# Block-sparse attention steps in a decoder layer: next logits placed behind the turn, keys and values fetched by separate transfers

## The chip, the cores and the metric

One core of a Trainium2 chip runs the kernel in one launch. Its engines work side by side and meet through semaphores: TensorE (PE, with its weight loads as PEld), VectorE (DVE), ScalarE (ACT), GpSimd (POOL) and SyncE (SP), which issues all transfers of this kernel; 16 DMA engines carry them. The metric is device time in microseconds (us), the median of several executions.

## What is computed

One layer of a hybrid decoder for a prompt of 512 tokens and for eight sequences of eight new tokens each (T = 576 rows in all), float32:

```python
xn = rmsnorm(x, ln1_g)
qa, ka, va, pb, gates = jnp.split(xn @ w_in, SPLIT_IN, axis=-1)
y_a = attend(qa, ka, va).reshape(B, T, WIDTH_A) @ w_br_a
y_b, wkv_new, shift_new = rwkv7_branch(pb, shift_prev, wkv0, mu, w0, w2, a0, a2, g2, k_k, k_a, r_k, lnx_g, lnx_b)
...
h = x + (g_a * y_a + g_b * y_b) @ w_o
u = rmsnorm(h, ln2_g) @ w_up
...
out = h + (jax.nn.silu(gt) * val) @ w_down
```

`attend` for the new tokens is block-sparse over a paged past of 4096 positions: for each head and token the 16 blocks of 256 positions are ranked by the product of the query with the block's mean key, and the softmax runs over the best three blocks and the new tokens:

```python
kmean = jnp.mean(k_full, axis=2)
gate = jnp.einsum('bthd,bjhd->bhtj', qf, kmean)
_, sel = lax.top_k(gate, n_sel)
...
probs = jax.nn.softmax(jnp.concatenate([lp for lp, _, _ in parts], axis=-1) * scale, axis=-1)
```

The prompt's attention (8 heads, 512 positions) and the RWKV-7 branch, a recurrence over the rows with a 64 x 64 state per head, need nothing from that cache.

## The kernel before, in words

The kernel has three parts: the input projections (to about 209 us), then 68 **block steps**, then the gates, output projection and feed-forward network. The change is in the block steps.

**The steps.** The eight sequences are taken in four pairs. A pair has 17 steps (`PER`): step 0 over its new tokens, then one for each of the 16 blocks of its past, so 68 in all (`STEPS`) and 64 of them with a block from the cache. Nothing is skipped: logits of every block are computed, their sum ranks the block, and the blocks' outputs are weighted later. A step i has these parts:

- `qk_step(i)` on PE (line 1019): logits of the block for all heads, into PSUM bank 7.
- `low_step(i)` on DVE (1944): the minimum of each row; `exp_step(i)` on ACT (1348): the exponentials; `gate_step(i)` on DVE (1951): the row sum of the logits for the ranking. Bank 7 is free for the next logits after both.
- `turn_step(i)` on PE (1033): the exponentials transposed; `pt_out(i)` on ACT (1375) copies them to SBUF.
- `pv_step(i)` on PE (1052): their product with the block's values; `o_out(i)` on ACT (1356) copies it out.

**The gaps.** Work of two other chains is put between these parts, at four places of a step called gap 0 to 3: on PE the order of step i is turn(i), gap 0, gap 1, values(i), logits(i+1), gap 2, gap 3. A gap takes one stage of the RWKV recurrence (`chunk_stage`, 157 in all: eight prompt chunks of 17 stages and 21 for the new tokens; within a chunk four gram stages, line 860, then pairs of level stages, lines 871 and 877 with 879, and three that close it), gaps 1 and 3 also one stage of the prompt's attention (`attention`, 48 in all: for each of 16 units logits, line 813, turn, 823, and values, 832). Successive stages of a chain depend on each other through a copy on ACT or an addition on DVE. Which stage stands in which gap is worked out by `layout()` (from line 213) from estimated costs; ACT and DVE follow the same table. `end_work` adds the later normalization of the recurrence's output (`EARLY_AT`, `LATE_AT`) and, in the last four steps, pieces of the first gate projections (line 667).

**The cache.** A block of a pair is a *fill*: four pages of 512 KB (two per sequence), each page 128 partitions of 2 KB of keys and 2 KB of values side by side. The fills go to a ring of three slots (`RING`). For each fill SP reads four page numbers from a table (line 578), waits until the values product of three fills earlier has released the slot, and issues four transfers (line 587), one per page. Four other loads and stores stand in this queue at fixed fills (`STATES_IN`, `STATES_OUT`, `X_IN`, `GATES_IN`); line 601 waits until the new states are stored before x is loaded again over them.

## Time and profile before

| | us |
|---|---|
| median of 3 runs (1301.61 to 1302.52) | 1301.92 |
| the profiled execution | 1303.04 |
| its span, first to last instruction | 1301.3 |
| PE busy | 1207.9 (93%) |
| PEld busy | 1099.4 (84%) |
| DVE busy | 618.0 (47%) |
| POOL busy | 434.4 (33%) |
| ACT busy | 413.9 (32%) |

The page divides the span into 40 slices of 32.5 us; the block steps lie in slices 7 to 20. In the rows below L587 is line 587 of the kernel; "<-" leads from what is written to what is read, or from a wait to what ended it; "x32" counts instructions. Share of busy time is an average over stages with different limits, so the steps are read by windows and by waits.

### The profile page before, as it was taken

The page shows a single profiled execution, that of the slowest core. Times are in us where ns is not written, and L with a number is a line of the kernel's source. Part 1 is how long each engine was busy: PE and PEld are TensorE (multiplying, and loading weights), DVE is VectorE, ACT ScalarE, POOL GpSimd, SP SyncE. Part 2 cuts the span into 40 slices and gives each one's busy share as a digit, 9 for nine tenths or more (in the row PEclk, how much of TensorE's full clock was granted, in tenths as well). Part 3 has the DMA queues.
Part 4 walks back from the last instruction along what each step waited for, and adds up shares of the span by engine and source line. Part 5 has one row for each costly group of instructions (what it writes and reads, how often), then busy time and mean ns, then how long its engine had stood idle before and what let it go on. Part 6 is the DMA issues. An engine that isn't in the chain of part 4 may idle for free. (4 is left out here: it accounts for less than half of the span.)

```text
span 1301.3 us, 33258 instructions
## 1 busy us (share of the span) xinstructions
PE 1207.9 (93%) x14362; PEld 1099.4 (84%) x14362; DVE 618.0 (47%) x1071; ACT 413.9 (32%) x773; POOL 434.4 (33%) x299
## 2 busy tenths in 40 slices
PE   6999998988899899887889999989999999999994
PEld 6998997766666667655689999989999999999994
DVE  6457896444555555674562222244444444440003
ACT  5142331333333333323522222333333333342110
POOL 3333453011101111010143333635555555564440
PEclk9999998999999999999899999989999999999998
DMA  5222215988798889789622222312222222222211
GB/s 212 98 102 66 80 53 227 388 332 326 274 378 318 296 329 376 269 291 378 227 81 82 82 82 82 114 44 82 82 82 82 82 82 83 96 88 88 90 58 73
DMA packets 57251, 216.28 MB, mean 166 GB/s; under 512 B 6609, under 2 KB 6994, under 8 KB 56338
## 3 DMA queue, kind: packets, MB, share of 16 engines
q1 hardware_dynamic: 57106, 214.17, 45.8%
q8 instruction: 113, 1.85, 0.6%
q14 instruction: 32, 0.26, 0.1%
HBM read 207.78 MB, written 6.37 MB: 165 GB/s over the span
## 5 line engine op out<-in xcount | busy, mean ns | idle before, releaser
L667 PE MATMUL ps<-buffer_at 128*128 128x288 f32 (+2 forms) x5760 | 778.4, 297 | 6.5 <-POOL buffer_at L1549 6.5
L667 PEld LDWEIGHTS ps<-buffer_at 128*128 128x128 f32 x5760 | 772.7, 190 | 13.0 <-POOL buffer_at L1549 7.2
L1549 POOL TENSOR_TENSOR buffer_at<-buffer_at 128x1024 fp32r<-128x1024 f32 (+1 forms) x118 | 331.8, 2814 | 340.1 <-ACT buffer_at L1254 339.5
L1254 ACT ACTIVATE buffer_at<-buffer_at 128x1024 fp32r<-128x1024 f32 (+1 forms) x118 | 129.2, 1097 | 287.6 <-PE ps L667 134.5
L1601 POOL TENSOR_TENSOR buffer_at<-buffer_at 128x256 f32<-128x256 f32 x45 | 40.4, 928 | 324.6 <-DVE buffer_at L1844 324.6
L1520 ACT ACTIVATE buffer_at<-buffer_at 128x592 f32<-128x592 f32 x44 | 38.9, 884 | 161.8 <-DVE buffer_at L2233 158.6
L2231 DVE TENSOR_TENSOR buffer_at<-ps,buffer_at 128x512 f32<-128x512 f32 x44 | 30.4, 692 | 125.6 <-PE ps L667 125.5
L1052 PE MATMUL ps<-buffer_at 128*32 128x128 f32 x2048 | 73.7, 283 | 15.5 <-ACT buffer_at L1375 8.7
L1944 DVE TENSOR_REDUCE buffer_at<-ps 128x1 f32<-128x256 f32 (+1 forms) x68 | 28.0, 412 | 103.2 <-PE ps L1019 103.1
L1019 PE MATMUL ps<-buffer_at 128*32 128x256 f32 x1024 | 72.6, 399 | 4.2 <-DMA buffer_at<-in_kvcache 2.9
L1052 PEld LDWEIGHTS ps<-buffer_at 128*32 128x32 f32 x2048 | 54.4, 112 | 25.0 <-issue 11.5
L2275 DVE TENSOR_TENSOR buffer_at<-buffer_at,ps 128x576 f32<-128x576 f32 x8 | 6.0, 755 | 121.7 <-PE ps L667 121.7
L1348 ACT ACTIVATE buffer_at<-ps,buffer_at 128x256 f32<-128x256 f32 (+1 forms) x68 | 31.7, 466 | 90.5 <-DVE buffer_at L1944 90.5
L1019 PEld LDWEIGHTS ps<-buffer_at 128*32 128x32 f32 x1024 | 34.4, 115 | 18.7 <-issue 9.4
L860 PEld LDWEIGHTS ps<-buffer_at 64*64 64x64 f32 x1152 | 38.1, 140 | 12.7 <-issue 8.8
L1637 POOL COPY buffer_at<-buffer_at 128x18 f32<-128x18 f32 x44 | 23.6, 535 | 72.3 <-DVE buffer_at L2233 72.3
L860 PE MATMUL ps<-buffer_at 64*64 64x64 f32 x1152 | 42.5, 226 | 4.0 <-DVEq L1834 2.6
L2243 DVE SCALAR_TENSOR_TENSOR buffer_at<-buffer_at 128x592 f32<-128x592 f32 x44 | 36.7, 835 | 18.8 <-ACT buffer_at L1520 18.8
L1356 ACT ACTIVATE buffer_at<-ps 128x128 f32<-128x128 f32 x68 | 18.9, 279 | 80.5 <-PE ps L1052 75.6
L1859 DVE TENSOR_TENSOR buffer_at<-buffer_at,ps 128x512 f32<-128x512 f32 x42 | 28.8, 686 | 25.3 <-PE ps L879 25.1
L2151 DVE TENSOR_TENSOR buffer_at<-ps,buffer_at 128x576 f32<-128x576 f32 x16 | 12.1, 758 | 60.3 <-PE ps L667 60.3
L871 PEld LDWEIGHTS ps<-buffer_at 64*64 64x64 f32 x672 | 23.0, 134 | 20.1 <-issue 11.1
(247 smaller groups left out, 1280.1 us busy)
## 6 DMA issues: line engine op xcount, KB each, us to landing
buffer_at<-in_kvcache SPq DMA_DIRECT2D x256, 512.0 KB, 6.0
buffer_at<-in_w_up SPq DMA_DIRECT2D x44, 512.0 KB, 3.5
buffer_at<-in_w_in SPq DMA_DIRECT2D x42, 512.0 KB, 3.5
buffer_at<-in_w_down SPq DMA_DIRECT2D x16, 704.0 KB, 4.1
buffer_at<-in_w_br SPq DMA_DIRECT2D x8, 512.0 KB, 3.5
buffer_at<-in_w_o SPq DMA_DIRECT2D x8, 512.0 KB, 3.5
buffer_at<-in_xin SPq DMA_DIRECT2D x4, 576.0 KB, 7.0
buffer_at<-in_xin SPq DMA_DIRECT2D x1, 2304.0 KB, 10.5
```

Of the source, the lines that this page charges most:

```text
L667: ins = e.matmul(out, lhs, rhs[:, cols], start=(start and i == 0), stop=(stop and i == 2))
L860: i = e.matmul(ps[r, k % 3, j * 256 + hp * C:j * 256 + (hp + 1) * C], lhs[r, hp, :], right, start=True, stop=True)
L1019: m_ = e.matmul(ps[32 * hp:32 * hp + 32, 7, 0:BLK], qbd[:, (2 * p + s) * HP + hp, :], kvring[slot_of(f)][:, 2 * s:2 * s + 2, hp * PAGE:(hp ...
L1052: m_ = e.matmul(ps[32 * hp:32 * hp + 32, 6, 0:P], pT[i % 2][:, k, 32 * hp:32 * hp + 32], kvring[slot_of(f)][:, k, WA + hp * P:WA + (hp + 1 ...
L1254: e.activation(hi[:, :, :], raw, ACT.Copy).then_inc(w_hi, 1)
L1348: e.activation(pe_[i % 2][:, 0:w], ps[:, 7, 0:w], ACT.Exp, bias=low[p % 2][:, j:j + 1], scale=-1.0, accum_out=esum[p % 2][:, j:j + 1]).the ...
L1520: e.activation(cc[s], cu[s][:, 2:594], ACT.Identity, bias=pcol("cb", col), scale=pcol("cw2", col)).then_inc(up_c0, 1)
L1549: e.tensor_tensor(lo[:, :, :], raw, hi[:, :, :], ALU.subtract).then_inc(w_lo, 1)
L1601: i = e.tensor_tensor(amt[:, l, :, :], aa[:, 1, :, :], mone("lvl", 128 + 64 * l), ALU.mult)
L1859: e.tensor_tensor(tt[:, :, :, :], tt[:, :, :, :], q8(2), ALU.add).then_inc(ch_te, 1)
L2231: e.tensor_tensor(cu[s][:, 2:514].rearrange("p (h n) -> p h n", h=2), ps[:, 2 * s:2 * s + 2, 0:256], rs[:, 0:512].rearrange("p (h n) -> p ...
L2243: ln.did(e.scalar_tensor_tensor(out=cc[s], in0=cu[s][:, 1:593], scalar=pcol("cw1", col), in1=cc[s], op0=ALU.mult, op1=ALU.add))
```

## The change

The change has four parts.

1. On PE the logits of step i+1 stand right behind the turn of step i, and the values of step i behind gaps 0 and 1. On ACT the exponentials and on DVE the minimum and the row sum move ahead accordingly.
2. Keys and values of a page are fetched by two transfers of 256 KB, each with its own semaphore. The four key transfers of a fill wait for the logits of three fills earlier, the four value transfers behind them for the values product of three fills earlier. PE waits for keys at the logits and for values at the values product.
3. `layout()` has other numbers: all 48 unit stages end in step 31 instead of 46, the last chunk stage is in step 61 instead of 60, and the stages for the new tokens' recurrence end in step 53 instead of 56.
4. `EARLY_AT` also waits for the last unit.

```diff
--- before
+++ after
@@ -217,10 +217,10 @@
     last_unit = None
     for i in range(STEPS):
         for part in range(4):
-            now += ((5, 2)[i % PER == 0], 0, (12, 4)[i % PER == 0] + (12, 3)[(i + 1) % PER == 0], 0)[part]
+            now += ((5, 2)[i % PER == 0] + (12, 3)[(i + 1) % PER == 0], 0, (12, 4)[i % PER == 0], 0)[part]
             for _ in range(1 + part % 2):
                 k = a // 3 % 4 + 1
-                if part % 2 and a < 3 * UNITS and (i, part) not in unit_at and unit_free <= now + 5 and 48 * a <= 3 * UNITS * (i + 1):
+                if part % 2 and a < 3 * UNITS and (i, part) not in unit_at and unit_free <= now + 5 and 32 * a <= 3 * UNITS * (i + 1):
                     if (i, part) in chunk_at:
                         break
                     work, pause = ((3 * k, 27 + 2 * k), (4 * k, 7 + 2 * k), (2 * k, 7))[a % 3]
@@ -230,7 +230,7 @@
                     a += 1
                     if a == 3 * UNITS:
                         last_unit = i
-                elif n < STAGES and (i, part) not in chunk_at and chunk_free <= now + (5 if last_unit is None else 8) and now + weight_of(n)[0] / 2 <= 40 + 16.5 * (4 * i + part + 1):
+                elif n < STAGES and (i, part) not in chunk_at and chunk_free <= now + 5 and now + weight_of(n)[0] / 2 <= 40 + 17.5 * (4 * i + part + 1):
                     if n >= SAMPLE_POS * CHUNK_STAGES + 8 and (last_unit is None or i < last_unit + 4):
                         continue
                     work, pause = weight_of(n)
@@ -255,7 +255,7 @@
 EARLY_T = (NCH - 1) * C
 LATE_T = T - EARLY_T
-EARLY_AT = {(max(i for (i, part), n in CHUNK_AT.items() if n < SAMPLE_POS * CHUNK_STAGES) + 1 + k, 2): k for k in range(10)}
+EARLY_AT = {(max(LAST_UNIT, max(i for (i, part), n in CHUNK_AT.items() if n < SAMPLE_POS * CHUNK_STAGES)) + 1 + k, 2): k for k in range(10)}
 LATE_AT = {(LAST_CHUNK + 1 + k // 2, 2 * (k % 2)): k for k in range(7)}
 STATES_IN, STATES_OUT, X_IN, GATES_IN = (fill_behind(i + 1) for i in (LAST_UNIT, SAMPLE_END, SAMPLE_END + 1, LAST_CHUNK))
...
@@ -578,14 +579,16 @@
                 found = [nc.values_load_multi_w_load_instructions(
                     ptab[0:1, (2 * p + s) * NPG + 2 * j:(2 * p + s) * NPG + 2 * j + 2], engines=(mybir.EngineType.SP,),
                     min_val=0, max_val=kvcache.shape[0] - 1)[1] for s in range(2)]
-                if f >= RING:
-                    e.wait_ge(sa_pv, fill_step(f - RING) + 1)
-                elif f == 0:
+                if f == 0:
                     e.wait_ge(p_tile, NR + NQ)
-                for s in range(2):
-                    for a, pg in enumerate(found[s]):
-                        e.dma_start(kvring[slot_of(f)][:, 2 * s + a, :],
-                                    kvcache[bass.ds(pg, 1)].rearrange("o p n -> p (o n)")).then_inc(kv_fill[slot_of(f)], 16)
+                for part, filled in ((0, k_fill), (1, vw_fill)):
+                    if f >= RING:
+                        e.wait_ge((sa_lg, sa_pv)[part], fill_step(f - RING) + 1)
+                    cols = slice(part * WA, (part + 1) * WA)
+                    for s in range(2):
+                        for a, pg in enumerate(found[s]):
+                            e.dma_start(kvring[slot_of(f)][:, 2 * s + a, cols],
+                                        kvcache[bass.ds(pg, 1)].rearrange("o p n -> p (o n)")[:, cols]).then_inc(filled[slot_of(f)], 16)
             for f in range(FILLS):
                 if f == STATES_IN:
...
@@ -1013,7 +1016,7 @@
                                           start=(s == 0), stop=(s == 1))
                 else:
                     f = step_fill(i)
-                    e.wait_ge(kv_fill[slot_of(f)], 64 * nth_fill(f))
+                    e.wait_ge(k_fill[slot_of(f)], 64 * nth_fill(f))
                     for s in range(2):
                         for hp in range(HP):
                             m_ = e.matmul(ps[32 * hp:32 * hp + 32, 7, 0:BLK], qbd[:, (2 * p + s) * HP + hp, :],
@@ -1047,6 +1050,7 @@
                                           vsm[0:NS, hp * P:(hp + 1) * P], start=(s == 0), stop=(s == 1))
                 else:
                     f = step_fill(i)
+                    e.wait_ge(vw_fill[slot_of(f)], 64 * nth_fill(f))
                     for k in range(4):
                         for hp in range(HP):
                             m_ = e.matmul(ps[32 * hp:32 * hp + 32, 6, 0:P], pT[i % 2][:, k, 32 * hp:32 * hp + 32],
@@ -1159,17 +1163,14 @@
             qk_step(0)
             for i in range(STEPS):
-                if i:
-                    turn_step(i)
+                turn_step(i)
+                if i + 1 < STEPS:
+                    qk_step(i + 1)
                 chunk_stage(CHUNK_AT.get((i, 0)))
                 end_work(i, 0)
                 attention(UNIT_AT.get((i, 1)))
                 chunk_stage(CHUNK_AT.get((i, 1)))
-                if i == 0:
-                    turn_step(i)
                 pv_step(i)
-                if i + 1 < STEPS:
-                    qk_step(i + 1)
                 chunk_stage(CHUNK_AT.get((i, 2)))
                 end_work(i, 2)
                 if i > PER and i % PER == 11:
@@ -1452,11 +1453,11 @@
                 attention(UNIT_AT.get((i - 1, 3)))
                 chunk_copies(CHUNK_AT.get((i, 0)))
                 end_work(i, 0)
+                if i + 1 < STEPS:
+                    exp_step(i + 1)
                 chunk_copies(CHUNK_AT.get((i, 1)))
                 attention(UNIT_AT.get((i, 1)))
                 o_out(i)
-                if i + 1 < STEPS:
-                    exp_step(i + 1)
                 chunk_copies(CHUNK_AT.get((i, 2)))
                 end_work(i, 2)
                 chunk_copies(CHUNK_AT.get((i, 3)))
...
@@ -2156,15 +2157,15 @@
                 att_second(UNIT_AT.get((i - 1, 3)))
                 chunk_out(CHUNK_AT.get((i, 0)))
                 end_work(i, 0)
+                if i + 1 < STEPS:
+                    low_step(i + 1)
                 att_first(UNIT_AT.get((i, 1)))
                 chunk_out(CHUNK_AT.get((i, 1)))
                 if i + 1 < STEPS:
-                    low_step(i + 1)
+                    gate_step(i + 1)
                 att_second(UNIT_AT.get((i, 1)))
                 chunk_out(CHUNK_AT.get((i, 2)))
                 end_work(i, 2)
-                if i + 1 < STEPS:
-                    gate_step(i + 1)
                 if p >= 0 and j == 11:
                     o_rows(p)
                 att_first(UNIT_AT.get((i, 3)))
```

What the queue of SP holds for one fill. Before (line 578 the page lookup, 587 the transfers, `s_pv` the count of values products; ISA rows are address arithmetic):

```order
L578 TENSOR_LOAD ptab
L578 ISA x4
L587 ISA [waits s_pv]
L587 DMA buffer_at<-in_kvcache 128x1024
L587 ISA
L587 DMA buffer_at<-in_kvcache 128x1024
L587 ISA
L587 DMA buffer_at<-in_kvcache 128x1024
L587 ISA
L587 DMA buffer_at<-in_kvcache 128x1024
```

And in the changed kernel, the end of the keys and the values of one fill with the lookup of the next (line 590 the transfers, 579 the lookup, `s_logits` the count of logits):

```order
L590 DMA buffer_at<-in_kvcache 128x512
L590 ISA [waits s_pv]
L590 DMA buffer_at<-in_kvcache 128x512
L590 ISA
L590 DMA buffer_at<-in_kvcache 128x512
L590 ISA
L590 DMA buffer_at<-in_kvcache 128x512
L590 ISA
L590 DMA buffer_at<-in_kvcache 128x512
L579 TENSOR_LOAD ptab
L579 ISA x4
```

Each fill has eight transfers of half the width in place of four, with the same lookups, and the wait for the values product stands between the fill's keys and its values, so the next fill's keys queue behind it too.

PE in the middle of the steps. Before (1033 turn, 1052 values, 1019 logits; 871 and 877 with 879 level stages of a chunk; 823 and 832 turn and values of a unit):

```order
L1033 MATMUL ps<-buffer_at 128x128 x2
L877 MATMUL ps<-buffer_at 64x64 x8
L879 MATMUL ps<-buffer_at 64x64 x8
L823 MATMUL ps<-buffer_at 128x128 x6
L871 MATMUL ps<-buffer_at 64x64 x8
L1052 MATMUL ps<-buffer_at 32x128 x16
L1019 MATMUL ps<-buffer_at 32x256 x8
L877 MATMUL ps<-buffer_at 64x64 x8
L879 MATMUL ps<-buffer_at 64x64 x8
L1033 MATMUL ps<-buffer_at 128x128 x2
```

And in the changed kernel, after step 32 (1036 turn, 1022 logits, 1056 values, 874 and 880 with 882 level stages):

```order
L1036 MATMUL ps<-buffer_at 128x128 x2
L1022 MATMUL ps<-buffer_at 32x256 x8
L880 MATMUL ps<-buffer_at 64x64 x8
L882 MATMUL ps<-buffer_at 64x64 x8
L1056 MATMUL ps<-buffer_at 32x128 x16
L874 MATMUL ps<-buffer_at 64x64 x8
L1036 MATMUL ps<-buffer_at 128x128 x2
L1022 MATMUL ps<-buffer_at 32x256 x8
```

The logits have moved from behind the values to behind the turn, and a step here holds two level stages and no unit.

## Rows read from the trace of the kernel before

**Rows 1.** The page, part 2: mean busy share of the 16 DMA engines in 40 slices.
```profile
DMA  5222215988798889789622222312222222222211
```

**Rows 2.** Windows: stretch, length, busy us (and instructions) of each engine, PEclk, DMA share, GB/s.
```profile
209.53:649.50 439.97, 387.86 (x8321) 290.54 (x8320) 238.92 (x532) 153.27 (x467) 47.62 (x51) 0.97 0.87 325
209.53:447.30 237.77, 211.89 (x4778) 161.26 (x4777) 121.70 (x287) 79.92 (x273) 29.45 (x33) 0.98 0.89 335
```

**Rows 3.** Waits of PE, 215 to 652 us: total us, times, longest.
```profile
PE ps L1033 <- ACT buffer_at L1348: 10.5, 20, 1.1
PE ps L1052 <- ACT buffer_at L1375: 8.7, 6, 3.6
...
PE ps L1019 <- DMA buffer_at<-in_kvcache: 2.9, 5, 0.8
```

**Rows 4.** Timeline of PE, 400 to 420 us: start, length, engine, line, operation.
```profile
404.49 1.05 PE L1019 MATMUL ps<-buffer_at 128*32 128x256 f32 x16
...
406.68 0.44 PE L1033 MATMUL ps<-buffer_at 128*128 128x128 f32 x2
...
407.86 0.68 PE L871 MATMUL ps<-buffer_at 64*64 64x64 f32 x16
...
408.47 1.08 PE L1052 MATMUL ps<-buffer_at 128*32 128x128 f32 x32
...
409.37 1.05 PE L1019 MATMUL ps<-buffer_at 128*32 128x256 f32 x16
...
410.34 0.68 PE L877 MATMUL ps<-buffer_at 64*64 64x64 f32 x16
...
411.56 0.44 PE L1033 MATMUL ps<-buffer_at 128*128 128x128 f32 x2
...
411.93 1.13 PE L813 MATMUL ps<-buffer_at 64*128 64x512 f32 x4
...
417.45 1.09 PE L823 MATMUL ps<-buffer_at 128*128 128x128 f32 x8
```

**Rows 5.** Waits of SP, 215 to 652 us: total us, times, longest.
```profile
SPq L587 <- PE ps L1052: 135.0, 57, 7.0
...
SPq L601 <- DMA out_wkvs<-buffer_at: 4.9, 1, 4.9
```

**Rows 6.** Timeline of SP: the first two fills and the fourth.
```profile
207.69 1.91 SPq L587 DMA_DIRECT2D buffer_at<-in_kvcache  x4
...
211.83 2.32 SPq L587 DMA_DIRECT2D buffer_at<-in_kvcache  x4
...
226.43 1.88 SPq L587 DMA_DIRECT2D buffer_at<-in_kvcache  x4
```

**Rows 7.** Line 587, all its transfers: ns min/median/max; us to landing.
```profile
L587 SPq DMA_DIRECT2D buffer_at<-in_kvcache x256: 332/333/1492, 207.7 to 633.3; - x128
...
DMA to landing us min/median/max: 3.2/6.0/10.9
```

**Rows 8.** Windows: 4 KB pieces alone; 4 KB pieces and x.
```profile
244.00:260.00 16.00, 14.84 (x366) 11.83 (x368) 7.02 (x18) 5.54 (x18) 0.07 (x1) 1.00 1.02 408
584.00:596.00 12.00, 10.35 (x230) 7.58 (x230) 5.86 (x13) 2.55 (x8) 0.00 (x0) 1.00 1.01 408
```

**Rows 9.** Timeline of PE, the last steps.
```profile
644.62 2.65 PE L667 MATMUL ps<-buffer_at 128*128 128x288 f32 x18
...
647.24 1.04 PE L667 MATMUL ps<-buffer_at 128*128 128x288 f32 x6
...
648.40 1.08 PE L1052 MATMUL ps<-buffer_at 128*32 128x128 f32 x32
```

**Rows 10.** Windows of 4 us in steps 61 to 64.
```profile
608.00:612.00 4.00, 2.78 (x60) 1.66 (x59) 1.12 (x2) 1.68 (x5) 0.00 (x0) 1.00 1.02 396
...
620.00:624.00 4.00, 3.15 (x48) 2.38 (x48) 1.38 (x6) 0.28 (x1) 0.00 (x0) 0.58 1.02 410
```

More of the change, by code:

```diff
@@ L502, in build @@
         s_c0, s_c1, s_pv, s_s0 = (sem(n) for n in ("ones_in", "const_in", "params_in", "states_in"))
+        in_slot = [64 * sum(slot_of(f) == i for f in range(FILLS)) for i in range(4)]
         s_x = sems("x_in", 4)
-        kv_fill = sems("kv_fill", RING)
-        w_a, w_g, w_u, w_d = sems("w_in", 4), sems("w_gate", 3), sems("w_up", 4), sems("w_down", 4)
+        k_fill = sems("k_fill", RING)
+        w_a, w_g, w_u, vw_fill = sems("w_in", 4), sems("w_gate", 3), sems("w_up", 4), sems("v_fill_w_down", 4)
         w_hi, w_lo, xh_ready, xs_even, xs_odd, hh_hi, hh_lo, yb_split, oa_split, st_stored = (sem(n) for n in (
@@ L647, in _ @@
                     e.wait_ge(dn_mm, i - 3)
-                e.dma_start(wd[i % 4], w_down[c][:, h * KH:(h + 1) * KH, :]).then_inc(w_d[i % 4], 16)
+                e.dma_start(wd[i % 4], w_down[c][:, h * KH:(h + 1) * KH, :]).then_inc(vw_fill[i % 4], 16)
             e.wait_ge(up_cp, 2 * NF)
@@ L1524, in _ @@
                 else:
-                    w_split(wdh[n - 2 * NF], wd[n - 2 * NF], w_d[n - 2 * NF], 16)
+                    w_split(wdh[n - 2 * NF], wd[n - 2 * NF], vw_fill[n - 2 * NF], in_slot[n - 2 * NF] + 16)
                 if q % 2:
@@ L1535, in _ @@
                 if i < 2 * KT:
-                    w_split(wdh[i % 4], wd[i % 4], w_d[i % 4], 16 * (i // 4 + 1))
+                    w_split(wdh[i % 4], wd[i % 4], vw_fill[i % 4], in_slot[i % 4] + 16 * (i // 4 + 1))
                 if i >= 4 and HALVES[i - 4][1]:
```

## The prediction

> **What bounds the kernel now.** I read the page's slices first, then the block steps by windows, then who waits for whom on PE and SP, then single stretches of the timeline. On the page the DMA share stands at 7 to 9 tenths in slices 7 to 20 [rows 1]. These are the 68 block steps: they run from 209.53 us to the end of the last values product, 648.40 + 1.08 = 649.48 us [rows 2, 9]. In these 440 us PE is busy for 387.9 us and idle for 52.1 [rows 2]. So at most 52 us are to be had there; before and after it nothing is moved.
>
> PE's waits in the steps [rows 3] are many and short: 10.5 us at the turn for the exponentials (20 times), 8.7 us at the values product for the turned copy, 2.9 us at the logits for the cache. The new order aims at the first two. In one step of the trace [rows 4] the turn takes 0.37 us to the start of what follows (411.56 to 411.93), values 0.90 (408.47 to 409.37), logits 0.97 (409.37 to 410.34): 2.24 us together. Between the start of the logits, 404.49 or 409.37, and the turn that needs them, 406.68 or 411.56, lie 2.19 us, which the work of one gap has to fill.
>
> The queue that loads the cache looks idle: SP waits 135.0 us for values products, 57 times [rows 5]. That is its whole slack, some 2.2 us for each of the 61 fills that have to wait. What a fill costs SP is seen where it waits for nothing, at the first fills [rows 6]: they start at 207.69 and 211.83, so 4.14 us for a clean one; four transfers take 1.91 us of it, the rest are the page lookups. The issue alone is 0.333 us [rows 7]; with its address work the step from one to the next is (1.88 - 0.33) / 3 = 0.52 us. One of the three quartets shown takes 2.32 instead of 1.88 to 1.91: a hiccup of 0.42, on average 0.14 per quartet.
>
> **The change part by part.** *The order.* Before, one or two gaps lie between logits and turn, and two between turn and values; now the logits have four gaps and the values product to hide their softmax behind, and the turn has the logits and two gaps. The 10.5 us and most of the 8.7 go. What is late next is the chunk chain: a stage in gap 0 and one in gap 1 stand with at most a unit stage between them, each needs ACT's or DVE's result of the one ahead, and on ACT and DVE the next block's exponentials and minimum are in between. And the logits of a unit stand in gap 3 for 15 of 16 units, their turn for twelve of these in gap 1 of the next step: turn, logits and a stage or two later, 2 to 4 us. In the trace the widest unit's logits ended at 411.93 + 1.13 = 413.06 and its turn could start at 417.45 [rows 4], 4.4 us; narrower ones I put at 3 to 4. These twelve places cost 0 to 1.8 us each, some 6 us together. The steps before the first states are there stay as they are. For the stretch up to step 30 I take 17 us of idle time; ends: 8 (the start and the tight units alone) and 25 (before had 237.8 - 211.9 = 25.9 in its first 38 steps [rows 2]).
>
> *The split transfers.* Each fill now issues eight. SP pays 4 x 0.52 = 2.06 us more: 4.14 + 2.06 = **6.20 us a fill**, and with a hiccup as often per issue as in [rows 6] 6.5. I take 6.5, since it is an issue that meets a hiccup; the ends are 6.2 and 6.7. Over 61 fills 2.06 us are 126 us of the 135 that SP waits. At the present pace SP has about 9 us left, and it cannot run a step below 6.2 us, where the old kernel had steps of 4.9 (turn to turn in [rows 4]). This term decides. What is gained: keys no longer wait for the values of their slot, so they are issued about a step earlier; that can be worth no more than the 2.9 us that PE waits for the cache.
>
> *The DMA engines.* A transfer is now 128 pieces of 2 KB. At full share they move 408 GB/s, in a stretch of 4 KB pieces alone and in one with the 18 KB pieces of x [rows 8]: 2 MB in 5.1 us. The trace shows no 2 KB pieces of the cache. As 18 KB and 4 KB make no difference, halving should cost at most a few per cent (5.4 us a fill); the other end, pieces that take as long as whole ones, is 10 us. I take 5.4, below SP's 6.5. The Trainium skill, page "DMA: Bandwidth & Descriptors", section "Rules for kernel authors", asks for at least 1 MiB per DMA and for small transfers to be put together, which speaks against this change; the full share that 512 KB transfers reach in this trace does not bear out that size, and by that rule the time would be that of the last rival but one below.
>
> *The layout.* All 48 unit stages end in step 31 (46 before); chunk stages fill three or four gaps of most steps up to there and two from step 32 on. PE's work for steps 0 to 31 comes from the stretch of before that holds nearly the same stages, 209.53 to 447.30: 211.9 us busy [rows 2]; less six steps' turn, logits and values (13.4), plus the nine unit stages not in it (about 0.8 each, the widest 1.13 and 1.09 [rows 4]: 7.1) and one level stage (410.34 to 411.56, 1.2): 206.8 us, 6.5 a step. For steps 32 to 67 387.9 - 206.8 = 181 us remain, 5.0 a step, and many hold two level stages only: 2.24 + 0.61 (407.86 to 408.47) + 1.22 = 4.1. So the first half runs at PE's pace; the second cannot, since SP needs 6.5.
>
> **The sum.** Up to the end of the values of step 30: 206.8 less step 31 (2.24, a unit's values 1.1, two level stages 1.8) and the last gaps of step 30 (two level stages and a unit's turn, 2.9) = 198.8 us of work, 17 idle, from 209.5: 425.3 us. There the values of fill 31 are issued (2.0: 427.3). From here SP has no wait left: fills 32 to 63 at 6.5 are 208 (635.3); the states, x and the first weights are seven issues of 0.52, 3.6; the wait for the stored states stays, 4.9 [rows 5]: the last issue is at 643.8. The last keys are issued 2.1 us ahead of it and land 3.2 us later (the shortest landing [rows 7]); behind them PE still has logits, two gate pieces of 1.04, one of 2.65, a turn and two values products, 0.97 + 2.08 + 2.65 + 0.37 + 0.90 + 1.08 = 8.1 us [rows 4, 9]. The steps end at 653.0 instead of 649.5: **+3.5 us**. From there on nothing changes. The profiled execution took 1303.0 (span 1301.3), 1.1 above the median; the median 1301.9 and 3.5 make **1305.4**. That is just beyond 0.2% (2.6 us), about what a measurement of this kernel can tell from no change.
>
> **The rivals.**
> *SP keeps up.* With fills of 6.2 and 10 us of idle time in the first half the sum loses 10 and 7 us: 1288; with either alone 1295 to 1298. For it: two of three quartets ran clean [rows 6], and the named waits of PE go for certain. Against it: 6.2 is a floor, and what SP waits in the heavy first half is lost. If SP did not count at all, half of the idle time, 26 us, might go. Chance 0.28.
> *The clock.* From step 32 on PE would work 4.1 us in a step of 6.5 and stand still in one piece. At 608 to 612 us PE was busy for 2.78 of 4 us, about as thin, and at 620 to 624 us the granted clock had gone from 1.00 to 0.58, turns of 2.4 and 1.2 GHz [rows 10]. At half the clock 4.1 us become 8.2, 1.7 more than SP needs. It decides once some seven of the 25 thin steps fall there and are not caught up: 12 us, 1317. Against it: SP runs ahead meanwhile, and the steps behind catch up. Chance 0.15.
> *DMA becomes the bound.* With 2 KB pieces at 300 GB/s a fill takes 7.0 us, 0.5 more than SP, over 32 fills 16 us: 1321. Against it: [rows 8]. Chance 0.07.
> *The waits only move.* PE now asks for keys right behind the turn, with two gaps and the values product queued behind that wait. If all that is saved comes back there, the time stays at 1302; this lies inside the forecast's own range.
>
> **How the numbers follow.** The forecast (PE's pace first, SP's later) has 0.50; its own range is 1297 to 1316, from idle 12 to 25 and fills of 6.4 to 6.7. Of it I give 0.28 to slower, 0.16 to no change, 0.06 to faster; the clock and DMA add 0.22 to slower, SP keeping up gives 0.25 to faster and 0.03 to no change. Slower 0.50, same 0.19, faster 0.31. The range reaches into both kinds of rivals: 1289 to 1319.
>
> **What would show it.** Right: SP's wait for values falls from 135 us to under 35, nearly all of it before step 32; PE's wait at the logits for the cache grows from 2.9 to 20 us or more, after step 32; the turn's 10.5 us are gone; steps 33 to 60 take 6.2 to 6.7 us each. Wrong: steps there below 6 us, SP still waiting in them, an issue step other than 0.52 us, or a DMA share near 10 tenths with fills landing later than now.

## The result, and the profile after

The changed kernel takes **1340.51 us** (median of 4 runs, 1335.06 to 1343.23) against 1302.22 for the kernel before in the same session: ratio 1.0279, 95% interval 1.0253 to 1.0305. The direction was forecast, the size was not: +38 us against +3.5, beyond the range. The profiled execution took 1342.16 us, its span is 1340.4. Of the twelve runs of e12 below, one took 2924.82 us and is left out of its median and ratio.

The page of the kernel after, part 2, the DMA engines' share (answers to [rows 1]):

```profile
DMA  5231217998789899999941222221222222222211
```

Nearly all the loss lies in the block steps. They end at 687.5 instead of 649.5 us; from there to the end it takes 652.9 us, before 651.8. Windows of the kernel after, the two halves of its steps (columns as in [rows 2]):

```profile
208.00:451.40 243.40, 214.66 (x4600) 159.62 (x4598) 123.96 (x286) 79.05 (x266) 30.16 (x34) 0.96 0.88 284
451.40:687.10 235.70, 192.83 (x3726) 137.94 (x3726) 115.14 (x248) 71.61 (x201) 18.56 (x17) 0.91 0.92 315
```

The second half, with little work in it, is as long as the first, and its clock is low. Waits of PE in the kernel after, 215 to 690 us (answers to [rows 3]; 1022 logits, 1036 block turn, 1033 the turn of a step over new tokens, 1056 values, 826 turn of a unit):

```profile
PE ps L1022 <- DMA buffer_at<-in_kvcache: 33.6, 16, 5.3
PE ps L826 <- DVE buffer_at L2057: 10.2, 8, 3.2
PE ps L1033 <- ACT buffer_at L1349: 3.9, 1, 3.9
PE ps L1036 <- ACT buffer_at L1349: 3.7, 5, 1.1
...
PE ps L1056 <- ACT buffer_at L1376: 2.2, 1, 2.2
```

The waits at the turn and at the values, 10.5 and 8.7 us before, have fallen to 3.7 and 2.2. The wait for the cache at the logits has grown from 2.9 to 33.6, of which 30.7 us come after 446 us. Waits of SP, same kernel, 205 to 690 us (answers to [rows 5]):

```profile
SPq L590 <- PE ps L1056: 21.7, 16, 7.3
...
SPq L598 <- DVE buffer_at L2064: 3.5, 1, 3.5
SPq L601 <- DVE buffer_at L1877: 3.4, 1, 3.4
```

SP's slack of 135.0 us has shrunk to 21.7. The timeline of SP shows what it does instead (start, length from first to last issue of a run, operation, count; a fill has 8):

```profile
208.73 17.72 SPq L590 DMA_DIRECT2D buffer_at<-in_kvcache  x24
...
230.40 215.22 SPq L590 DMA_DIRECT2D buffer_at<-in_kvcache  x232
449.22 0.34 SPq L598 DMA_DIRECT2D buffer_at<-in_s0t  x1
451.79 138.81 SPq L590 DMA_DIRECT2D buffer_at<-in_kvcache  x168
593.98 0.35 SPq L601 DMA_DIRECT2D out_wkvs<-buffer_at  x1
...
606.23 46.61 SPq L590 DMA_DIRECT2D buffer_at<-in_kvcache  x56
...
657.56 16.33 SPq L590 DMA_DIRECT2D buffer_at<-in_kvcache  x24
```

With one more lookup (2.05 us) added, the run of 29 fills took (215.22 + 2.05) / 29 = 7.5 us a fill, the next, of 21 fills, 6.7, the one of seven 7.0. The shortest time in the trace from the first issue of a fill to that of the next is 6.16 us, the clean 6.20 of the prediction; the median is 6.97. A single issue is as before, and a transfer of half the size lands in 4.6 us instead of 6.0 (median; answers to [rows 7]):

```profile
L590 SPq DMA_DIRECT2D buffer_at<-in_kvcache x512: 332/333/1863, 208.7 to 673.6; - x171
...
DMA to landing us min/median/max: 2.7/4.6/9.4
```

How the wait for keys reaches PE shows in a step of the second half (timeline of PE, 552 to 560 us, in brackets the wait and its end):

```profile
552.79 0.44 PE L1036 MATMUL ps<-buffer_at 128*128 128x128 f32 x2
554.71 1.07 PE L1022 MATMUL ps<-buffer_at 128*32 128x256 f32 x16 [1.48 <-DMA buffer_at<-in_kvcache]
...
556.90 1.08 PE L1056 MATMUL ps<-buffer_at 128*32 128x128 f32 x32
...
559.11 0.44 PE L1036 MATMUL ps<-buffer_at 128*128 128x128 f32 x2
```

The turn is on time; the logits right behind it wait for keys, and a stage of the new tokens' recurrence (lines 948 and 950, left out above) and the values stand behind them in PE's queue. The step from turn to turn is 6.32 us. Single steps differ widely: from step 33 to 60 they take 3.6 to 12.2 us, 6.6 on average, and 14 of the 27 are below 6.

### The profile page after: what moved, and what is told of

Its sections match the earlier page's. It is cut to its first block and busy times, and to the rows that moved or that the text cites. A ratio compares the mean times of both kernels' runs of the same rounds, so it can differ in the third digit from the quotient of the medians.

```text
span 1340.4 us, 34029 instructions
## 1 busy us (share of the span) xinstructions
PE 1228.3 (92%) x14362; PEld 1107.3 (83%) x14362; DVE 625.5 (47%) x1071; ACT 411.4 (31%) x773; POOL 433.5 (32%) x299
## 5 line engine op out<-in xcount | busy, mean ns | idle before, releaser
L1022 PE MATMUL ps<-buffer_at 128*32 128x256 f32 x1024 | 77.3, 414 | 35.8 <-DMA buffer_at<-in_kvcache 33.6
L1022 PEld LDWEIGHTS ps<-buffer_at 128*32 128x32 f32 x1024 | 30.5, 114 | 59.9 <-issue 50.8
L1056 PEld LDWEIGHTS ps<-buffer_at 128*32 128x32 f32 x2048 | 54.6, 113 | 13.7 <-issue 7.6
L863 PEld LDWEIGHTS ps<-buffer_at 64*64 64x64 f32 x1152 | 39.6, 145 | 12.4 <-issue 9.4
L1376 ACT ACTIVATE buffer_at<-ps 128x256 f32<-128x256 f32 x64 | 24.5, 382 | 65.6 <-PE ps L1036 65.3
L1952 DVE TENSOR_REDUCE buffer_at<-ps 128x1 f32<-128x256 f32 x64 | 27.0, 422 | 34.7 <-ACT buffer_at L1349 34.6
L2152 DVE TENSOR_TENSOR buffer_at<-ps,buffer_at 128x576 f32<-128x576 f32 x16 | 12.1, 757 | 61.1 <-PE ps L670 61.1
```

The source lines that it names most:

```text
L863: i = e.matmul(ps[r, k % 3, j * 256 + hp * C:j * 256 + (hp + 1) * C], lhs[r, hp, :], right, start=True, stop=True)
L1022: m_ = e.matmul(ps[32 * hp:32 * hp + 32, 7, 0:BLK], qbd[:, (2 * p + s) * HP + hp, :], kvring[slot_of(f)][:, 2 * s:2 * s + 2, hp * PAGE:(hp ...
L1056: m_ = e.matmul(ps[32 * hp:32 * hp + 32, 6, 0:P], pT[i % 2][:, k, 32 * hp:32 * hp + 32], kvring[slot_of(f)][:, k, WA + hp * P:WA + (hp + 1 ...
```

## The experiments

Four theories stood to be told apart. **1**: the issuing queue, SP with eight issues a fill, sets the pace. **2**: the DMA engines do, through pieces of 2 KB. **3**: the layout costs, with its full first half and thin second. **4**: the order costs, by itself or by asking for keys earlier. All ratios are to the kernel before on the same chip, with 95% intervals. Edits are to the kernel before unless another base is named. They are shortened: `<page>` stands for the page's address, dots for what is left out, and the counts of semaphores that follow from an edit are not shown.

### The transfers, one property at a time

**e1**, eight issues with pieces of 4 KB:

```diff
+for h in (slice(0, P // 2), slice(P // 2, P)):
-    e.dma_start(kvring[slot_of(f)][:, 2 * s + a, :], <page>).then_inc(kv_fill[slot_of(f)], 16)
+    e.dma_start(kvring[slot_of(f)][h, 2 * s + a, :], <page>[h, :]).then_inc(kv_fill[slot_of(f)], 16)
```

> The kernel before, with each page fetched as two transfers of 64 partitions by 4 KB: eight issues a fill as in the change, the same 4 KB pieces, one wait and one semaphore as before. Theory 1 (the issuing queue: eight issues of 0.52 us and 2 us of lookups make 6.2 us a fill, with late issues some 6.7, against a mean step of 6.8 us): SP's wait for values falls from 135 us to under 50, PE waits for the cache at the logits 15 us and more, time 1315 to 1340. Theory 2 (the DMA engines need longer for 2 KB pieces): the pieces are the old ones, so 1299 to 1306. Theories 3 (the layout) and 4 (the order of logits and values): neither is touched, 1299 to 1306.

Measured: 1440.37 us, ratio 1.1002 (1.0947 to 1.1058), far beyond every theory. Windows of this kernel (330 to 700 us), and its transfers:

```profile
330.00:700.00 370.00, 287.96 (x5731) 211.69 (x5727) 159.50 (x366) 93.91 (x299) 30.21 (x34) 0.90 1.01 241
```
```profile
L588 SPq DMA_DIRECT2D buffer_at<-in_kvcache x512: 468/469/1645, 208.4 to 779.4; - x171
...
DMA to landing us min/median/max: 3.4/8.0/16.6
```

At full DMA share only 241 GB/s move, where pieces of the same size to all partitions reach 408 [rows 8]. A transfer to half the partitions is slow in itself, so this run brought a new cost with it and says nothing on SP. e8 asks its question without that cost.

**e2**, four issues with pieces of 2 KB (keys and values of a page as two blocks in memory):

```diff
-e.dma_start(kvring[slot_of(f)][:, 2 * s + a, :], kvcache[...].rearrange("o p n -> p (o n)"))
+e.dma_start(kvring[slot_of(f)][:, 2 * s + a, :].rearrange("p (t n) -> p t n", t=2),
+            kvcache[...].rearrange("o t p n -> p (o t) n"))
```

> The kernel before, with keys and values of a page as two blocks in memory, so that each of the four transfers of a fill has pieces of 2 KB, as in the change, at half the issues. Theory 1 (issuing queue): four issues as before, SP's wait for values stays near 135 us, time 1299 to 1306. Theory 2 (DMA engines, pieces): a fill takes up to a tenth longer to land, the share of the DMA engines rises over 0.9 at the same rate, PE waits for the cache 15 us and more, time 1310 to 1340. Theories 3 and 4: 1299 to 1306.

Measured: 1310.19 us, 1.0048 (1.0024 to 1.0071). Windows of this kernel, the stretch of [rows 8], and its waits of SP:

```profile
244.00:260.00 16.00, 15.11 (x366) 11.98 (x370) 7.14 (x18) 5.66 (x18) 0.06 (x1) 1.00 1.05 384
```
```profile
SPq L587 <- PE ps L1052: 132.8, 53, 6.5
```

Small pieces do move more slowly in this stretch, 384 against 408 GB/s, a loss of 6%. While SP has its slack that costs half a per cent: theory 2 is a small part.

**e8**, eight issues and 2 KB pieces to all partitions, behind the one old wait:

```diff
+for h in (slice(0, WA), slice(WA, 2 * WA)):
     for s in range(2):
         for a, pg in enumerate(found[s]):
-            e.dma_start(kvring[slot_of(f)][:, 2 * s + a, :], <page>)
+            e.dma_start(kvring[slot_of(f)][:, 2 * s + a, h], <page>[:, h])
```

> The kernel before, with each page fetched as two transfers of all partitions, key half and value half, behind one wait for the values three fills back: eight issues and 2 KB pieces as in the change, the wait of before. Small pieces alone gave 1.005. Theory 1 (issuing queue): SP becomes the bound as in the split alone and the last issue comes 4.1 us behind the wait where it was 2.1, so 1320 to 1345. Theory 2 (DMA engines alone): as the small pieces, 1305 to 1313.

Measured: 1334.01 us, 1.0224 (1.0191 to 1.0257). Waits of SP and PE in this kernel:

```profile
SPq L588 <- PE ps L1053: 12.9, 10, 4.0
```
```profile
PE ps L1020 <- DMA buffer_at<-in_kvcache: 28.0, 17, 3.9
```

With 2 KB pieces at four issues the loss was 0.5%, at eight it is 2.2%: the other 1.8% comes with the four more issues. Theory 1.

**e3**, the transfers of the change whole, so with keys waiting for the logits alone (item 2 of the change, on the order and layout of before; `w_d`, a semaphore of later weights, counts the values):

```diff
+for part, filled in ((0, kv_fill), (1, w_d)):
+    if f >= RING:
+        e.wait_ge((sa_lg, sa_pv)[part], fill_step(f - RING) + 1)
```

> The kernel before, with the change's transfers alone: keys and values of a page by transfers of their own, keys waiting for the logits three fills back and values for the values three fills back; order on PE, ACT and DVE and layout as before. Theories 1 and 2 (issuing queue, DMA engines): the price is in the transfers, so most of the 38 us is here, 1320 to 1342, SP's wait for values under 40 us. Theories 3 and 4 (layout, order): the transfers alone cost nothing, 1299 to 1308.

Measured: 1322.26 us, 1.0122 (1.0094 to 1.0150). Keys that are asked for earlier, and logits that wait for keys alone, win back 1.0 of e8's 2.2%. The split alone accounts for some 16 of the 38 us.

### Order and layout

**e4**, the change with whole pages behind one wait (item 2 undone); **e7**, that with the layout of before as well, so the order alone; **e6**, the change with the layout of before:

```diff
 e4: -for part, filled in ((0, k_fill), (1, vw_fill)): ...
     +e.wait_ge(sa_pv, fill_step(f - RING) + 1)
     +e.dma_start(kvring[slot_of(f)][:, 2 * s + a, :], <page>).then_inc(k_fill[slot_of(f)], 16)
 e6: -... 32 * a <= 3 * UNITS * (i + 1) ... chunk_free <= now + 5 and ... 17.5 * (4 * i + part + 1)
     +... 48 * a <= 3 * UNITS * (i + 1) ... chunk_free <= now + (5 if last_unit is None else 8) and ... 16.5 * (4 * i + part + 1)
 e7: both
```

> The change, with its order and its layout, but whole pages again: four transfers a fill behind one wait for the values three fills back. Theories 1 and 2 (issuing queue, DMA engines): SP's wait for values is back at over 100 us and the time comes most of the way to before, 1298 to 1312; above that only if the shorter time from the freeing of a slot to its next logits (some one and a half steps in place of two) is now missed, which shows as PE waiting for the cache right behind the turn. Theories 3 and 4 (layout, order): the time stays at 1330 to 1345 and the SP wait is back, too.

> The kernel before, with the order of the change alone: logits of the next step right behind the turn, whole pages behind one wait, layout by the numbers of before. Theory 4 (order): a slot is freed by the values of three fills back and wanted by the logits one and a half steps later, where it was two: PE waits for the cache at the logits 40 us and more, 1325 to 1370. Theory 3 (the layout was the cost, and the order is neutral or a gain): 1295 to 1310, the wait of 10.5 us at the turn gone.

> The change, with the stages and units laid out by the numbers of before (units up to step 46 again); order and split transfers as in the change. Theory 3 (the crowded first half and the thin second one cost the 17 us that the split alone does not explain): the time falls to that of the split alone, 1318 to 1328, the step work per stretch is even again, the clock is over 0.97. Theory 4 (logits right behind the turn): it stays at 1333 to 1350, PE waits at the logits and at the units' turn.

Measured: e4 1366.74 us, 1.0448 (1.0405 to 1.0490); e7 1350.34, 1.0364 (1.0312 to 1.0417); e6 1330.22, 1.0212 (1.0188 to 1.0236). Waits in e7, of SP and of PE:

```profile
SPq L588 <- PE ps L1053: 184.3, 56, 9.3
```
```profile
PE ps L1020 <- DMA buffer_at<-in_kvcache: 58.1, 28, 4.2
```

Whole pages made it worse, which neither theory 1 nor theory 2 had as its first reading. Here SP has slack, 184.3 us, and PE waits 58.1 us for the cache: the logits want a page sooner after its slot came free than it has landed. So the split was not the mistake; with this order it is worth 1.5% (e7 to e6). The layout costs 0.7 to 0.8% (e6 to the change, e7 to e4). The order on top of the split costs 0.9% (e3 to e6). All these prices hold with the two lookups of the change; with cheaper ones they are others (below).

### What the order is worth with free supply

**e9** (order of the change, layout of before), **e10** (order and layout of before) and **e17** (order and layout of the change) fetch keys only, after the first three fills. The values of later fills are left out, so the output is not the layer's:

```diff
 if f >= RING:
+    if part:
+        continue
-    e.wait_ge((sa_lg, sa_pv)[part], fill_step(f - RING) + 1)
+    e.wait_ge(sa_lg, fill_step(f - RING) + 1)
```

> The order of the change with the layout of before, and after the first three fills no values are fetched (the values products reuse the old ones, so the output is not the reference's): half the bytes, four issues a fill. It asks what the order is worth where the supply of pages limits nothing, beside the next run. Theories 1 and 2 (supply): PE's wait for the cache under 4 us, no wait at the block turn, 1283 to 1297, below the next run by the waits of 10.5 and 8.7 us or part of them. Theory 4 (the order itself costs): 1305 to 1325, the time now at the units or at other waits behind the turn.

> Order and layout of before, and after the first three fills no values are fetched, as in the run before this one (the output is not the reference's). The supply hardly limited the kernel before (2.9 us of waiting for the cache), so 1295 to 1304 by every theory; it is the base for the run before it.

> The change with order and layout, and after the first three fills no values are fetched (the output is not the reference's): half the bytes. If the layout costs only because its thin second half outruns the DMA engines (theory 2 through the layout), it is level with the order alone at half the bytes, 1274 to 1284. If it costs by itself (theory 3: the unit turns' wait for DVE of 10 us, the clock), 1288 to 1305, with no wait for the cache to speak of. Theory 1 has half the issues here and nothing left to charge.

Measured: e9 1278.00 us, 0.9801 (0.9771 to 0.9831); e10 1287.55, 0.9878 (0.9848 to 0.9907); e17 1287.66, 0.9859 (0.9843 to 0.9876). Waits of PE in e9, in e10, and in e17 (1058 values, 1038 block turn, 1024 logits, 828 turn of a unit in all three):

```profile
PE ps L828 <- DVE buffer_at L2059: 4.2, 5, 2.4
PE ps L1058 <- ACT buffer_at L1378: 4.1, 3, 1.8
...
PE ps L1024 <- DMA buffer_at<-in_kvcache: 3.2, 2, 1.6
...
PE ps L1038 <- ACT buffer_at L1351: 2.1, 2, 1.4
```
```profile
PE ps L1038 <- ACT buffer_at L1354: 12.3, 23, 1.4
PE ps L1058 <- ACT buffer_at L1381: 8.1, 6, 3.1
```
```profile
PE ps L828 <- DVE buffer_at L2059: 12.1, 12, 3.2
```

e9 and e10 are both lower than any theory put them: supply costs the old kernel more than I had read. e17 lies just under the range of theory 3. The order is good: e9 is 10 us below e10, half of the two waits it aims at. Theory 4 in its bare form falls. Theory 3 holds in part: the layout takes 0.6% of that back even with free supply (e9 to e17). The units' turn waits 12.1 us in e17 and 4.2 in e9; that this is the whole reason is not shown. e10 is 16 us below the kernel before, whose named wait for the cache is 2.9 us; in its steps PE is idle for 41.3 us instead of 52.1 and busy for 381.3 instead of 387.9. What the rest of these 16 us is was not separated.

### Relieving the queue

**e5**, the change with one lookup of four page numbers a fill (which stand side by side in the table for it), and **e11**, the same on e3 (split alone):

```diff
-found = [nc.values_load_multi_w_load_instructions(ptab[0:1, <two numbers of sequence s>], ...)[1] for s in range(2)]
+four = nc.values_load_multi_w_load_instructions(ptab[0:1, 4 * f:4 * f + 4], ...)[1]
+found = [four[0:2], four[2:4]]
```

> The change, with the page numbers of a fill side by side in the table, so that SP looks them up by one load of four where it had two loads of two; transfers, order and layout as in the change. Theory 1 (the issuing queue bounds the steps; the clean period of a fill was 6.17 us, 2.05 of it lookups): the period falls by 0.7 to 1.0 us, PE's wait for the cache at the logits from 33.6 to under 15 us, time 1308 to 1328. Theory 2 (the DMA engines): the same bytes in the same pieces, 1335 to 1345. Theories 3 and 4 (layout, order): 1335 to 1345 with less waiting for the cache and more elsewhere.

> Order and layout of before, the split transfers, and one lookup of four page numbers a fill. Theory 1 (issuing queue): the split alone cost 1.2%; the single lookup gave 14 us on top of the change, so here 1303 to 1312, PE's wait for the cache under 12 us. Theory 2 (DMA engines, pieces of 2 KB at a share over 0.9): the lookup gives nothing, 1316 to 1326.

Measured: e5 1325.97 us, 1.0169 (1.0138 to 1.0200), shortest period of a fill 5.49 instead of 6.16 us; e11 1304.07, 0.9996 (0.9967 to 1.0025). Nothing but SP's own time was touched, and 1.1 to 1.2% came back each time: theory 1 shown directly. For the split alone that is the whole loss, for the change some 14 of its 38 us. In e5 the cache wait fell only to 26.4 us, not under 15 as theory 1 expected.

**e13** (order of the change, split, layout of before), **e14** (the whole change), **e15** (split alone) and **e16** (the kernel before) have the cheapest lookup, the single load of e5 without the range tests on SP:

```diff
-    min_val=0, max_val=kvcache.shape[0] - 1)[1]
+    min_val=0, max_val=kvcache.shape[0] - 1, skip_runtime_bounds_check_because=...)[1]
```

> Order and split transfers of the change, layout of before, and the cheapest lookup: one load of four page numbers a fill, without the range tests on SP (the table holds numbers of pages of the pool). SP's period of a fill should fall from 6.2 to 4.5 to 5.0 us. Theory 1 (only the issuing queue stood in the way): PE's wait for the cache falls from 31.7 to under 12 us, 1290 to 1304, at or below before. Theory 2 (DMA engines, 2 KB pieces, share over 0.9): the queue waits for slots again but the pages land late, 1306 to 1320. Theory 4 (the order costs by itself): 1310 to 1322 with little waiting for the cache.

> The change with its own layout, and the cheapest lookup as in the run before this one. Theory 1: 1295 to 1312. Theory 3 (the layout costs on its own): 10 to 20 us above the run before this one, PE waiting at the units' turn (10.2 us in the change) and for the cache in its second half. Theory 2: 1315 to 1328.

> Order and layout of before with split transfers and the cheapest lookup: the base of e13 for the order alone. The split with one lookup stood level with before, and its wait for the cache was 4.4 us, so little is left to win: 1296 to 1305. If this is level with e13, the order is worth nothing while all the bytes are fetched; if e13 is 8 us and more below, it is worth what it was with half the bytes.

> The kernel before with the cheapest lookup and nothing else. Its queue waited 135 us for slots, and the lookups stand ahead of that wait, so by every theory 1299 to 1306; a gain of over 4 us would say that even the kernel before was held by the queue.

Measured: e13 1299.30 us, 0.9960 (0.9940 to 0.9979); e14 1325.13, 1.0151 (1.0123 to 1.0180); e15 1299.04, 0.9953 (0.9930 to 0.9975); e16 1305.15, 0.9999 (0.9983 to 1.0016). e13's first three fills on SP, and its waits of SP and PE:

```profile
207.39 13.62 SPq L591 DMA_DIRECT2D buffer_at<-in_kvcache  x24
```
```profile
SPq L591 <- PE ps L1057: 93.9, 44, 6.6
```
```profile
PE ps L1023 <- DMA buffer_at<-in_kvcache: 7.9, 10, 1.8
```

13.62 us where the change took 17.72; SP waits for slots again, and the same order and transfers that lost 2.1% (e6) are now 0.4% below before. On e16, whose queue had slack, the lookup does nothing. That e13 is only level with e15 says that with all bytes the order's 10 us are not had at this pace of supply. e14 stays 1.5% above before, although its queue waits for slots as e13's does:

```profile
SPq L591 <- PE ps L1057: 104.2, 39, 8.9
```

It is 26 us above e13, in the range of theory 2. That theory comes in here through the layout; its windows from the start of the second half:

```profile
451.40:560.00 108.60, 92.59 (x2148) 68.61 (x2144) 52.55 (x118) 29.42 (x94) 9.01 (x10) 0.97 1.00 361
```

Over this stretch the DMA engines are at their full share on average: the thin half now asks faster than they bring. Its waits of PE, 452 to 680 us and 215 to 452 us:

```profile
PE ps L1023 <- DMA buffer_at<-in_kvcache: 13.9, 7, 4.8
```
```profile
PE ps L827 <- DVE buffer_at L2058: 12.5, 11, 3.2
```

With a relieved queue the layout costs 1.9% (e13 to e14), with half the bytes 0.6%. So most of its price goes with the bytes. I read it thus: the first half leaves bandwidth unused (share 0.88 and 0.83 in the two halves of 208 to 451 us, e13 0.97 and 0.94), and the second is short of it. The part of the clock (below) was not taken out: in its steps PE is busy for 402.5 us in e14 and for 389.6 in e13.

### A version that beats both

**e12** exchanges logits and values alone, on the kernel before; **e18** does that on e15.

```diff
-pv_step(i)
 if i + 1 < STEPS:
     qk_step(i + 1)
+pv_step(i)
...
-o_out(i)
 if i + 1 < STEPS:
     exp_step(i + 1)
+o_out(i)
```

> The kernel before with one exchange: the logits of the next step stand just ahead of the values of this step, not behind them (on ACT the next exponential ahead of this step's output); whole pages, layout as before. If the waits of before at the turn (10.5 us) and at the values (8.7 us) are what the order can win, and the slot is wanted only some 1.2 us earlier: 1288 to 1300. If supply decides here too (theories 1 and 2), PE's wait for the cache rises from 2.9 to over 10 us and it stays at 1300 to 1312.

> Layout of before, split transfers, the cheapest lookup, and the logits of the next step just ahead of this step's values (as in e12, where the waits at turn and values went and 23.8 us of waiting for the cache came). If the issuing queue was what stood against it (theory 1): 1288 to 1298, the waits at the turn and at the values gone, the cache wait under 8 us. If the DMA engines hold all orders alike while all bytes are fetched (theory 2): 1296 to 1304, as the order and the split were with the same lookup.

Measured: e12 1306.72 us, 1.0022 (0.9997 to 1.0046); e18 1291.67, **0.9891** (0.9874 to 0.9907). Waits of PE in e12, then of SP and PE in e18:

```profile
PE ps L1019 <- DMA buffer_at<-in_kvcache: 23.8, 16, 5.0
PE ps L1019 <- DVE buffer_at L1951: 7.8, 3, 3.3
```
```profile
SPq L591 <- PE ps L1057: 75.8, 37, 4.9
```
```profile
PE ps L1023 <- DMA buffer_at<-in_kvcache: 3.6, 4, 1.9
```

In e12 the waits of 10.5 and 8.7 us went, and 23.8 us of waiting for the cache and 7.8 for the row sum of the logits before (bank 7 is still being read) took their place: even the time of one values product, some 1 us, is too early for whole pages. With split transfers and the relieved queue the exchange is worth 0.6% over e15, by the ratios, since the two ran on different chips, and 1.1% in all.

## Why the prediction was wrong

**Bound and mechanism: right for the second half.** The turn's and the values' waits went, SP's slack fell below 35 us, and the cache wait passed 20 us. From 446 us on SP waits for values for 2.9 us only and PE for the cache for 30.7, so there PE is held at SP's pace. e5 and e11 show that the queue costs time, e2 that pieces of 2 KB are a small cost; the forecast's 5.4 us a fill on the DMA engines stands beside 2.1 MB / 384 GB/s = 5.5. SP's remaining wait lies before step 32, as forecast (18.8 of 21.7 us up to 446). The steps behind it take 6.5 to 6.6 us on average (values of step 30 end at 441.2 us, of 45 at 538.1, of 60 at 636.9), but this sign tells little: before, steps 31 to 60 took 6.6 as well. And one sign of being wrong came, too, the many steps below 6 us.

**The sizes failed, at four terms.** Against the profiled execution the forecast was 1303.0 + 3.5 = 1306.5, and 1342.2 came, 35.7 more:

- *"The first half runs at PE's pace"*: +18.3 us. The values of fill 31 are issued at 445.6 us (end of the run of 232 above), not at 427.3. This is the step that failed first: PE's own pace was put too fast, by 7.4 us of work and 8.5 of idle time. Windows up to the end of the values of step 30, in the change, in e14 (the change with the relieved queue) and in e17 (the change with keys alone):

```profile
209.50:441.25 231.75, 206.22 (x4425) 152.95 (x4425) 119.08 (x277) 75.34 (x255) 30.07 (x34) 0.96 0.89 289
```
```profile
209.50:437.60 228.10, 205.57 (x4425) 152.98 (x4423) 118.46 (x277) 75.41 (x255) 29.83 (x34) 0.95 0.87 293
```
```profile
209.50:428.30 218.80, 199.58 (x4424) 149.06 (x4422) 118.13 (x277) 75.51 (x255) 29.56 (x34) 0.98 0.55 176
```

  The sum had 198.8 us of work. In e17, at a granted clock of 0.98, the same instructions keep PE busy for 199.6, in the change, at 0.96, for 206.2: the work was counted right for the clock of its source (0.98 in [rows 2]), and a lower clock was left out. Of idle time the sum had 17, and 25.5 came. The units' turn is 10.2 of it, where I had 6, and the turn of step 0, which has moved ahead of its gaps, 3.9; the wait for the cache is 2.9. Last, SP was itself late at this point: the last issue comes 4.4 us after the values of step 30, not 2.0. So in the first half the queue is the smaller part of the miss: with SP waiting 104.2 us for slots in e14 the values of step 30 still end at 437.6, in e5 at 434.8, each in one profiled execution. Why e17 is another 6 to 9 us faster is open; its half bytes go with a higher clock and 19.2 us of idle time. In e3, with layout and order of before and thus steps of 6.3 us, the queue does hold the first half: there the values of step 30 end at 417.7 us, 404.7 before, and in e11, with the cheaper lookup, at 403.5.
- *"Fills 32 to 63 at 6.5"*: +11.8 us, 228.3 from there to the last issue (673.9) where the sum had 216.5. The runs of the timeline show 6.7 and 7.0. Late issues cost more than I had: 61 of the 512 took over 0.36 us, and together they cost 0.5 us a fill, where 6.5 - 6.2 had left 0.3. The trace of before would have told, with 26 of 256 and 0.25 us for four issues; three quartets were too few. The load of the states stopped SP for 3.5 us, for which the sum had nothing, when it had no slack left to make that up (for the store, 3.4, it had 4.9). In e5, with the cheaper lookup, the same stretch took 218.0.
- *The tail*: +4.4 us, 13.6 from the last issue to the end of the steps, not 9.2. The cause was not looked into.
- *After the steps*: +1.1 us, 652.9 against 651.8, where "nothing changes" stood.

**The layout's price** was in the sum only as thin steps held by SP. e6 gives it 0.7%, and e17 shows 0.6% that stays with half the bytes.

**The rivals.** "SP keeps up" is refuted. "DMA becomes the bound" is refuted as the first bound of the change (e5 wins without touching a byte) and comes true in the second half of e14. "The clock" came as a part; windows of the kernel after, a stretch of the second half and all the steps:

```profile
611.00:623.00 12.00, 6.74 (x100) 4.96 (x98) 2.19 (x6) 1.50 (x5) 0.00 (x0) 0.72 1.02 384
```
```profile
209.50:687.50 478.00, 407.24 (x8324) 297.35 (x8324) 238.59 (x533) 150.70 (x467) 48.91 (x52) 0.94 0.90 300
```

In the stretch PE was busy for 6.74 of 12 us, and the granted clock, 0.72 on average, shows turns of 2.4 and 1.2 GHz. In all the steps PE was busy for 407.2 us, before for 387.9 with the same instructions and a clock of 0.97 [rows 2]. That is 19 us, half of the 38; against the sum 7.4 of them stand up to the end of step 30, where PE hardly waits for the cache, and 12 behind it. How much of them was on the path, no run separates. How longer work follows on a wait shows in one step of the kernel after (timeline of PE, then a window of its end):

```profile
505.93 1.22 PE L1022 MATMUL ps<-buffer_at 128*32 128x256 f32 x16 [3.00 <-DMA buffer_at<-in_kvcache]
...
508.98 1.61 PE L1056 MATMUL ps<-buffer_at 128*32 128x128 f32 x32
```
```profile
508.00:510.50 2.50, 2.50 (x52) 2.12 (x50) 1.02 (x2) 0.34 (x1) 0.00 (x0) 0.57 0.89 250
```

PE stood still for 3.00 us, then the granted clock averaged 0.57, and the values took 1.61 us instead of the 1.08 of the step above.

**The rule on transfer size.** By the Trainium skill, page "DMA: Bandwidth & Descriptors", section "Rules for kernel authors", which asks for 1 MiB and more per DMA, the change goes the wrong way. The direction agrees; the runs put 0.5% on the smaller pieces (e2) and 1.8% on the number of issues (e8 to e2).

## What to carry to other kernels

A queue that "waits 135 us" has slack only while its own time per item is well below the consumer's. Take that time as the mean of all its items, late ones included (6.2 us clean and 0.5 for late issues here), and compare it with the consumer's pace in each part: in e3, with steps of 6.3 us, it cost 13 us by step 30. And a wait can cost more than its length, where the clock falls behind it: here the same work kept PE busy for 19 us longer. Before splitting a transfer, count what its issuer spends per item besides the issues: here the page lookups were a third of a fill, and making them cheap was worth as much as the split cost. An order that asks earlier for data is worth its hidden latency only if the supply is early too, so try it once with the supply halved, to see what it can give.

## What the runs showed of the hardware

Three things I had not expected. Transfers to 64 partitions of 4 KB moved 241 GB/s at full DMA share against 408 for 128 partitions, and each issue took 0.469 us instead of 0.333 (e1). The Trainium skill, page "DMA: Bandwidth & Descriptors", section "Rules for kernel authors", advises one transfer over 128 partitions in place of two to disjoint halves; the trace agrees. Pieces of 2 KB to all partitions moved 384 GB/s at full share where pieces of 4 KB moved 408 (e2, 6%). And the two lookups of a fill with their range tests hold SP for 2.05 us, as long as four issues: in one load and without the tests the shortest period of a fill fell from 6.16 to 4.53 us (e13).
